# Keys-low product of the second attention's scores over all 128 rows

## The chip, the cores and the metric

The kernel runs on one core of one Trainium2 chip. The metric is the device time of one execution in microseconds (us), the median over the runs shown. TensorE (PE) does the matrix products, VectorE (DVE), ScalarE (ACT) and GpSimd (POOL) the elementwise work, and SyncE (SP) issues the transfers. All matrices are in SBUF, and TensorE writes to the eight banks of PSUM, 512 float32 columns each.

## The reference

The reference is a decoder trunk with two layers on a sequence of 512 tokens, with 1024 channels. Layer one is a causal attention with forget gates, then a squared-ReLU MLP. Layer two is a sliding-window attention that reads one shared set of keys and values, then another such MLP. The change is in layer two's attention. Cut to what matters:

```
q = rmsnorm((h @ w_q).reshape(512, 16 heads, 64), g_q)
k, v = shared keys and values: 2 heads of 64, each read by 8 query heads
s = q . k / sqrt(64) + bias(distance)          # previous block of 128 and the own one
s = -inf outside the window of 128
p = softmax([s, sink])                          # the sink logit is dropped afterwards
o = (p @ v) @ w_out
```

## The kernel before

Nearly all products are made in a rounded float32 format that TensorE takes at full rate. To keep float32 precision, a matrix is held as two parts: *hi* is the rounded value, *lo* the rounded rest. A large product is three of them (function `three`, lines 1210 to 1212): hi by hi, hi by lo, lo by hi. The weight projections and the MLPs are made so, with 512 moving columns each.

**Second attention.** The 16 query heads are done as 8 pairs j = 0 to 7, and a head of a pair is e = 0 or 1. A head has 64 channels, and SBUF has 128 partitions, so the two parts of one head share a tile. `q_hl[:, e, :]` holds the hi part of head e's queries on the 64 rows `own`, which are rows 0 to 63 for e = 0 and 64 to 127 for e = 1, and the lo part on the 64 others. `kd_hi[:, g, :]` holds the hi part of key head g twice, on both halves of the rows, and `kd_lo[:, g, :]` the lo part twice, likewise.

**Scores** (`swa_scores`). For head e there are four key blocks kb of 128 keys. Each has 256 queries, and the last has 128. The scores of a key block are the sum of five products in PSUM: keys hi by queries hi and lo at once over 128 rows (line 1554), keys lo by queries hi over 64 rows (line 1555), minus the row maximum through a diagonal matrix (line 1556), and the bias in two parts (lines 1557, 1558). After the four blocks, one product of 512 columns (line 1561) puts the maximum into bank 6 + e and signals `swa_scores_done`. It may write this bank only after the output of the previous pair's head has been taken from it (`swa_out_stored`, set by DVE on line 1173).

**Order on PE.** The order is written out by hand. For each pair j it is: `swa_max_scores(j)` (rough scores over 64 rows, lines 1532 to 1539, for the row maximum), the projection of pair j+2 (`swa_proj`, 24 products of 512 columns and 2 of `swa_sum`), `swa_scores(j)`, `swa_pv(j)` (probabilities by values, line 1570, 7 products of 128 columns for each head; the trace merges the 14 products of a pair and their 14 weight loads into one row of x28). In pairs 6 and 7 there is no projection left, and a piece of 12 products of the output projection (`out_piece`) stands in its place. In pair 0 half of a projection stands there.

**Other engines.** DVE does for pair j: the row maxima (`swa_max`, lines 1147 to 1153), the diagonal matrix of each head (line 1157, `swa_diag_ready`), the end of the previous pair's reciprocal (lines 990, 993), the previous pair's output (line 1173, one instruction for each head), the norm of a later pair's queries (lines 830, 833, 1106), then the lo part of the next queries (line 1114) and the denominators (line 1166). ACT does the exponentials of head 0 and head 1 after each `swa_scores_done` (lines 738, 739, 741), and with the last of them lets `swa_pv` begin. Then it makes the hi part of the next queries (line 731), the start of the reciprocal (lines 596, 598) and, after pairs 1, 3 and 5, the hi part of a weight unit (line 469), whose lo part POOL makes (line 410).

Weights come in units of 1 MB through two slots. Each transfer, hi part and lo part waits for the use of a unit before it.

Of the kernel before, what the change touches and what calls it, by code (L numbers as in the profile page):

```python
# [90 lines left out]
def build(nc, x, g_attn, g_mlp, w_in_a, b_f, gq_a, gk_a, w_out_a, g_kv, w_kv, gk_b,  # L91
          w_q_b, gq_b, sinks, rel_bias, w_out_b, w_up, w_down, consts, out):
    with ExitStack() as ctx:
# [6 lines left out]
        def at(name, shape, dt, offset):  # L100
            assert offset + 4 * int(np.prod(shape[1:])) <= limit, (name, offset, limit)
            return nc.alloc_sbuf_tensor_at(name, shape, dt, offset=offset)
# [83 lines left out]
        q_hl = at("q_hl", [P, 2, T], F32R, area + 61 * KB)  # L186
        kd_hi = at("kd_hi", [P, 2, T], F32R, area + 65 * KB)
        kd_lo = at("kd_lo", [P, 2, T], F32R, area + 69 * KB)
# [111 lines left out]
        def after(eng, s, count):  # L300

            if not (isinstance(count, int) and count <= 0):
                eng.wait_ge(s, count)
# [901 lines left out]
        def _(pe):  # L1205
            mm = nc.tensor.matmul
# [27 lines left out]
            for v in range(4):  # L1234
# [7 lines left out]
                for k in range(KC):  # L1242
# [19 lines left out]
                    for b in range(TB):  # L1262
                        o = ps[:, V_BANKS[v] + b // 2, 256 * (b % 2):256 * (b % 2) + 256]
# [278 lines left out]
            def swa_scores(j):  # L1542
                g = j // (PAIRS // 2)
                pe.wait_ge(swa_lo_ready, j + 2)
                for e in range(2):
                    pe.wait_ge(swa_diag_ready, 2 * j + e + 1)
                    b = 2 + 2 * e
                    h = slice(64 * e, 64 * e + 64)
                    for kb, bank, c0 in ((0, b, 0), (1, b, 256), (2, b + 1, 0), (3, b + 1, 256)):
                        n = 2 * P if kb < TB - 1 else P  # L1550
                        o = ps[:, bank, c0:c0 + n]
                        ks, qs = slice(kb * P, (kb + 1) * P), slice(kb * P, kb * P + n)

                        mm(o, kd_hi[:, g, ks], q_hl[:, e, qs], start=True, stop=False)
                        mm(o, kd_lo[h, g, ks], q_hl[h, e, qs], start=False, stop=False)  # L1555
                        mm(o, ones_r[:], swa_diag[:, e, qs], start=False, stop=False)  # L1556
                        mm(o, anti_r[:], hk_lo[:, 2 * j + e, 0:n], start=False, stop=False)  # L1557
                        mm(o, anti_r[:], hk_hi[:, 2 * j + e, 0:n], start=False, stop=True)

                    after(pe, swa_out_stored, 2 * j - 1 + e)  # L1560
                    mm(ps[:, 6 + e, :], ones_r[:], swa_diag[:, e, :], start=True, stop=True).then_inc(swa_scores_done, 1)
# [21 lines left out]
            for j in range(PAIRS - 1):  # L1583
                swa_max_scores(j)
                if j == 0:
                    swa_proj(2, False, (2, 6), range(4, KC))
                elif j + 2 < PAIRS:
                    swa_proj(j + 2, False, (j + 2, 2))
                if j == 6:
                    pe.wait_ge(swa_raw_ready, PAIRS + 1)  # L1590
                    out_piece(1, 0, range(1), range(0, 4))
                    swa_sum(PAIRS)
                if j == 0:
                    pe.wait_ge(swa_v_ready, 1)
                    pe.wait_ge(hankel_lo_ready, 1)
                if j == PAIRS // 2:
                    pe.wait_ge(hankel_lo_ready, 2)
                swa_scores(j)
                swa_pv(j)
            swa_max_scores(PAIRS - 1)  # L1600
            pe.wait_ge(swa_rstd_refined, 2 * PAIRS + 1)
            out_piece(1, 0, range(1, 2), range(0, 4))
            swa_scores(PAIRS - 1)
            swa_pv(PAIRS - 1)
            out_piece(1, 0, both, range(4, 7))
# [44 lines left out]
```

## Time and profile before

| | |
|---|---|
| device time, median of 3 runs | 1274.31 us (1271.7 to 1276.66) |
| span of the profiled execution | 1267.8 us |
| PE busy | 1226.4 us, 97% of the span |
| DVE, ACT, POOL busy | 576.1, 478.2, 558.5 us |
| mean granted TensorE clock over the span | 0.984 of full |

The span runs from the first to the last instruction of the profiled execution. The profile gives no device time of that execution; what lies around the span is taken as 1274.31 - 1267.8 = 6.5 us. The granted clock is a share of 2.4 GHz, so 1.00 is 2.4 GHz and 0.50 is 1.2 GHz. The ends of matmuls are modelled, and consecutive ones overlap in the trace, so the pace of TensorE is read from one start to the next, not from durations.

### The profile page before, as it was taken

What the parts mean: (1) busy time and instruction counts of PE and PEld (TensorE: products, weight loads), DVE (VectorE), ACT (ScalarE), POOL (GpSimd) and SP (SyncE); (2) the same over time, 40 slices, a digit from 0 to 9 for tenths busy, and PEclk for the clock granted to TensorE, in tenths of its full rate; (3) what the DMA queues carried; (4) which work ended last, traced back from release to release, by engine and by line L of the source; (5) the groups of instructions that cost most, each with busy time, mean ns of one, the idle gap of its engine ahead of it and who ended that gap; (6) DMA issues with size and microseconds to landing.
All of it is one profiled execution on the core that took longest, in us unless ns stands there. A gap on an engine that the chain in (4) does not pass through costs nothing.

```text
span 1267.8 us, 15311 instructions
## 1 busy us (share of the span) xinstructions
PE 1226.4 (97%) x5794; PEld 1010.5 (80%) x5794; DVE 576.1 (45%) x717; ACT 478.2 (38%) x594; POOL 558.5 (44%) x383
## 2 busy tenths in 40 slices
PE   6999999999999999999999799999999999999998
PEld 6877877777888888888887678777788888888887
DVE  5857778867533001333116676866743200133100
ACT  4248778753322112222227244443332211222221
POOL 4513423415655444565445320221655544566532
PEclk9999999999999999999999699989999999999999
DMA  6221211112333353333333101110333333323341
GB/s 219 80 66 34 55 45 33 59 41 69 99 99 99 100 166 99 94 92 83 97 99 100 34 1 33 34 34 1 100 100 99 100 100 99 91 89 92 103 116 42
DMA packets 142238, 101.24 MB, mean 80 GB/s; under 512 B 3128, under 2 KB 141552, under 8 KB 142192
## 3 DMA queue, kind: packets, MB, share of 16 engines
q1 hardware_dynamic: 142128, 100.56, 26.8%
q8 instruction: 32, 0.52, 0.2%
q14 instruction: 14, 0.11, 0.0%
q10 hardware_dynamic: 64, 0.03, 0.0%
HBM read 98.47 MB, written 2.12 MB: 79 GB/s over the span
## 4 chain that ended last, share of the span: by engine, by line
PE 68%; issue 15%; DVE 7%; POOL 6%; ACT 3%; DMA 0%; SPq 0%; POOLq 0%; ACTq 0%; DVEq 0%
PE ps L1210 21%; PE ps L1212 21%; PE ps L1211 21%; POOL w_lo L410 5%; POOL fox_sq_lo L417 1%; PE ps L1556 1%; PE ps L1555 1%; DVE xn_lo L854 1%; DVE rst L826 1%; DVE x_hat L847 1%; DVE swa_diag L1157 1%; PE ps L1570 1%; ACT w_hi L469 1%; DMA x_in<-in_x 0%; PE ps L1557 0%
## 5 line engine op out<-in xcount | busy, mean ns | idle before, releaser
L410 POOL TENSOR_TENSOR w_lo<-stage,w_hi 128x512 fp32r<-128x512 f32 x356 | 519.9, 1490 | 487.8 <-ACT w_hi L469 480.2
L469 ACT ACTIVATE w_hi<-stage 128x2048 fp32r<-128x2048 f32 x88 | 168.4, 1914 | 475.2 <-PE ps L1212 470.4
L1210 PE MATMUL ps<-xn_hi,w_hi 128*128 128x512 f32 x720 | 285.3, 396 | 0.3 <-issue 0.3
L1212 PE MATMUL ps<-xn_hi,w_lo 128*128 128x512 f32 x720 | 281.0, 390 | 0.0
L1211 PE MATMUL ps<-xn_lo,w_hi 128*128 128x512 f32 x720 | 280.9, 390 | 0.0
L1210 PE MATMUL ps<-r_hi,w_hi 128*128 128x512 f32 x512 | 199.8, 390 | 0.0
L1212 PE MATMUL ps<-r_hi,w_lo 128*128 128x512 f32 x512 | 199.3, 389 | 0.0
L1211 PE MATMUL ps<-r_lo,w_hi 128*128 128x512 f32 x512 | 199.2, 389 | 0.0
L1210 PEld LDWEIGHTS ps<-xn_hi,w_hi 128*128 128x128 f32 x720 | 135.5, 188 | 30.6 <-issue 2.7
L1211 PEld LDWEIGHTS ps<-xn_lo,w_hi 128*128 128x128 f32 x720 | 135.5, 188 | 29.2 <-issue 1.9
L1212 PEld LDWEIGHTS ps<-xn_hi,w_lo 128*128 128x128 f32 x720 | 135.4, 188 | 28.6
L1035 DVE TENSOR_TENSOR hT<-hT,ps 128x512 f32 x40 | 26.8, 685 | 231.5 <-PE ps L1212 231.5
L1057 DVE SCALAR_TENSOR_TENSOR qkn<-ps,rst 128x1024 f32<-128x1024 f32 x32 | 39.2, 1225 | 186.3 <-PE ps L1212 185.8
L1212 PEld LDWEIGHTS ps<-r_hi,w_lo 128*128 128x128 f32 x512 | 96.1, 188 | 20.2
L1211 PEld LDWEIGHTS ps<-r_lo,w_hi 128*128 128x128 f32 x512 | 96.1, 188 | 19.8
L1210 PEld LDWEIGHTS ps<-r_hi,w_hi 128*128 128x128 f32 x512 | 96.1, 188 | 19.7
L417 POOL TENSOR_TENSOR fox_sq_lo<-sqt,fox_sq_hi 128x512 fp32r<-128x512 f32 x14 | 20.6, 1474 | 105.7 <-ACT fox_sq_hi L556 105.5
L1064 DVE TENSOR_TENSOR r_lo<-sqt,r_hi 128x1024 f32 x32 | 52.6, 1643 | 19.0 <-ACT r_hi L675 18.7
L417 POOL TENSOR_TENSOR swa_sq_lo<-sqt,swa_sq_hi 128x512 fp32r<-128x512 f32 x6 | 7.9, 1316 | 94.8 <-ACT swa_sq_hi L714 94.8
L826 DVE TENSOR_TENSOR rst<-rst,sqt 128x512 f32<-128x512 f32 x32 | 41.3, 1289 | 17.3 <-ACT sqt L479 16.7
L854 DVE SCALAR_TENSOR_TENSOR xn_lo<-hT,gains,xn_hi (+1 forms) x40 | 47.7, 1204 | 1.8 <-ACT xn_hi L506 1.8
L479 ACT ACTIVATE sqt<-hT 128x512 f32 (+1 forms) x32 | 19.7, 622 | 71.7 <-DVE hT L1035 65.8
(208 smaller groups left out, 1716.9 us busy)
## 6 DMA issues: line engine op xcount, KB each, us to landing
stage<-in_w_up SPq DMA_DIRECT2D x32, 1024.0 KB, 5.5
stage<-in_w_down SPq DMA_DIRECT2D x32, 1024.0 KB, 5.7
stage<-in_w_in_a SPq DMA_DIRECT2D x16, 512.0 KB, 5.0
stage<-in_w_in_a SPq DMA_DIRECT2D x4, 1024.0 KB, 6.2
stage<-in_w_out_a SPq DMA_DIRECT2D x4, 1024.0 KB, 5.2
stage<-in_w_q_b SPq DMA_DIRECT2D x4, 1024.0 KB, 5.1
stage<-in_w_out_b SPq DMA_DIRECT2D x4, 1024.0 KB, 5.2
x_in<-in_x SPq DMA_DIRECT2D x4, 512.0 KB, 7.3
```

The source lines that it names most:

```text
L410: ins = nc.gpsimd.tensor_tensor(w_lo[:, s, c], stage[:, s, c], w_hi[:, s, c].bitcast(F32), ALU.subtract)
L417: nc.gpsimd.tensor_tensor(lo[:], sqt[:, t, :], hi[:].bitcast(F32), ALU.subtract).then_inc(split, 1)
L469: nc.scalar.activation(w_hi[:, s, :], stage[:, s, :], ACT.Copy).then_inc(w_hi_ready, 1)
L479: nc.scalar.activation(sqt[:, slot, :], src, ACT.Square).then_inc(norm_squared, 1)
L826: V.tensor_tensor(acc, acc, sqt[:, slot, :], ALU.add).then_inc(norm_accumulated, 1)
L854: V.scalar_tensor_tensor(out=one[2], in0=one[0], scalar=gains[:, bass.ds(8 * GAIN[fill] + c, 1)], in1=one[1].bitcast(F32), op0=ALU.mult, o ...
L1035: V.tensor_tensor(dst, dst, ps[:, bank, :], ALU.add).then_inc(h_written, 1)
L1057: V.scalar_tensor_tensor(out=qkn[:], in0=ps[:, 2 * j:2 * j + 2, :], scalar=0.0, in1=scale, op0=ALU.max, op1=ALU.mult).then_inc(u_ready, 1)
L1064: V.tensor_tensor(r_lo[:, bass.ds(2 * i, 2), :], sqt[:], r_hi[:, bass.ds(2 * i, 2), :].bitcast(F32), ALU.subtract).then_inc(r_lo_ready, 1)
L1210: mm(out_, st_hi, mv_hi, start=start, stop=False)
L1211: mm(out_, st_hi, mv_lo, start=False, stop=False)
L1212: return mm(out_, st_lo, mv_hi, start=False, stop=stop)
```

## The change

The second of the five products of a key block, keys lo by queries, takes all 128 rows of both tiles instead of the 64 rows of head e's hi queries. Its sum then also has keys lo by queries lo. The number of instructions stays, as do the columns, all tiles, all waits and signals. The slice `h` is no longer needed in this function.

```diff
                 for e in range(2):
                     pe.wait_ge(swa_diag_ready, 2 * j + e + 1)
                     b = 2 + 2 * e
-                    h = slice(64 * e, 64 * e + 64)
                     for kb, bank, c0 in ((0, b, 0), (1, b, 256), (2, b + 1, 0), (3, b + 1, 256)):
                         n = 2 * P if kb < TB - 1 else P
                         o = ps[:, bank, c0:c0 + n]
                         ks, qs = slice(kb * P, (kb + 1) * P), slice(kb * P, kb * P + n)
 
                         mm(o, kd_hi[:, g, ks], q_hl[:, e, qs], start=True, stop=False)
-                        mm(o, kd_lo[h, g, ks], q_hl[h, e, qs], start=False, stop=False)
+                        mm(o, kd_lo[:, g, ks], q_hl[:, e, qs], start=False, stop=False)
                         mm(o, ones_r[:], swa_diag[:, e, qs], start=False, stop=False)
                         mm(o, anti_r[:], hk_lo[:, 2 * j + e, 0:n], start=False, stop=False)
                         mm(o, anti_r[:], hk_hi[:, 2 * j + e, 0:n], start=False, stop=True)
```

## Rows read from the trace of the kernel before

**Rows 1.** The page: busy time by engine, and the chain that ended last by engine.
```profile
PE 1226.4 (97%) x5794; PEld 1010.5 (80%) x5794; DVE 576.1 (45%) x717; ACT 478.2 (38%) x594; POOL 558.5 (44%) x383
...
PE 68%; issue 15%; DVE 7%; POOL 6%; ACT 3%; DMA 0%; SPq 0%; POOLq 0%; ACTq 0%; DVEq 0%
```
**Rows 2.** Line 1555's instructions: ns min/median/max, starts, forms.
```profile
L1555 PE MATMUL ps<-q_hl,kd_lo x64: 322/381/580, 710.6 to 866.0; 64*128 64x256 f32 x48, 64*128 64x128 f32 x16
```
**Rows 3.** Timeline of PE, pair 1 head 0: start us, us, instruction.
```profile
736.46 0.28 PE L1554 MATMUL ps<-q_hl,kd_hi 128*128 128x256 f32 x1
736.66 0.38 PE L1555 MATMUL ps<-q_hl,kd_lo 64*128 64x256 f32 x1
736.97 0.38 PE L1556 MATMUL ps<-swa_diag,ones_r 128*128 128x256 f32 x1
737.19 0.28 PE L1557 MATMUL ps<-hk_lo,anti_r 128*128 128x256 f32 x1
737.31 0.28 PE L1558 MATMUL ps<-hk_hi,anti_r 128*128 128x256 f32 x1
737.43 0.28 PE L1554 MATMUL ps<-q_hl,kd_hi 128*128 128x256 f32 x1
...
740.19 0.44 PE L1561 MATMUL ps<-swa_diag,ones_r 128*128 128x512 f32 x1
740.47 0.28 PE L1554 MATMUL ps<-q_hl,kd_hi 128*128 128x256 f32 x1
...
744.49 3.63 PE L1570 MATMUL ps<-swa_p,swa_vx 128*128 128x128 f32 x28
```
**Rows 4.** Timeline of PE, scores of the first attention, all 128 rows.
```profile
272.01 0.28 PE L1340 MATMUL ps<-qk_hi 128*128 128x256 f32 x1
272.13 0.28 PE L1341 MATMUL ps<-qk_x 128*128 128x256 f32 x1
```
**Rows 5.** Timeline of PE, pair 0: first product, then `swa_pv`; brackets give idle time before.
```profile
710.14 0.55 PE L1554 MATMUL ps<-q_hl,kd_hi 128*128 128x256 f32 x1 [6.79 <-DVE swa_diag L1157]
...
723.98 4.18 PE L1570 MATMUL ps<-swa_p,swa_vx 128*128 128x128 f32 x28
```
**Rows 6.** Stretches at the low clock: us, busy us (instructions) of PE, clock, DMA.
```profile
57.04:60.10 3.06, 3.06 (x14) 0.50 0.02 5
268.66:271.50 2.84, 2.84 (x9) 0.50 0.00 0
710.14:723.98 13.84, 13.84 (x42) 0.50 0.00 0
```
**Rows 7.** Timeline of DVE: diagonals and outputs in pairs 1, 2 and 7.
```profile
735.50 1.41 DVE L1173 TENSOR_TENSOR o_t<-ps,q_rec 64x512 f32<-64x512 f32 x2
...
754.80 1.74 DVE L1157 TENSOR_TENSOR swa_diag<-kept,nm 128x512 fp32r<-128x512 f32 x1
...
759.96 1.41 DVE L1173 TENSOR_TENSOR o_t<-ps,q_rec 64x512 f32<-64x512 f32 x2
...
860.76 1.41 DVE L1173 TENSOR_TENSOR o_t<-ps,q_rec 64x512 f32<-64x512 f32 x2
```
**Rows 8.** Timeline of PE: line 1561 of head 0 in pairs 2, 6, 7, and pair 6's `swa_pv`.
```profile
760.70 0.50 PE L1561 MATMUL ps<-swa_diag,ones_r 128*128 128x512 f32 x1 [0.40 <-DVE o_t L1173]
...
841.66 0.61 PE L1561 MATMUL ps<-swa_diag,ones_r 128*128 128x512 f32 x1 [3.08 <-DVE o_t L1173]
...
848.93 4.83 PE L1570 MATMUL ps<-swa_p,swa_vx 128*128 128x128 f32 x28
...
862.61 0.44 PE L1561 MATMUL ps<-swa_diag,ones_r 128*128 128x512 f32 x1
```
**Rows 9.** Timeline of ACT, pair 1 head 0: the last exponential.
```profile
741.53 0.69 ACT L741 ACTIVATE psink<-ps,sinkb 128x512 f32<-128x512 f32 x1
```
**Rows 10.** Timeline of PE: idle before a product at 1.2 GHz, and before one at 2.4 GHz.
```profile
57.04 0.55 PE L1210 MATMUL ps<-w_hi,xn_hi 128*128 128x256 f32 x1 [2.25 <-DVE v_all L908]
...
888.65 0.47 PE L1210 MATMUL ps<-ob_hi,w_hi 128*128 128x512 f32 x1 [1.75 <-POOL w_lo L410]
```

## The prediction

> **What bounds the kernel now.** I read the page first. TensorE is busy for 97% of the span, the others for less than half, and the chain that ended last lies 68% on TensorE, with another 15% as its issue [rows 1]. So time taken off TensorE counts, if the stage around it has no other limit. Busy time hides how it is spent: matmuls overlap in the trace. Next I took the instructions of the changed line, to count them: 64, of which 48 have 256 columns and 16 have 128 [rows 2]. Then I read the timeline of TensorE through a pair of heads, from start to start, and saw the point of the whole case. Two products over 128 rows that follow each other start 0.12 us apart (line 1557 to 1558, and 1558 to the next block's 1554). Around the 64-row product the distances are 0.20 (1554 to 1555), 0.31 (1555 to 1556) and 0.22 us (1556 to 1557) [rows 3]. One block of five products takes 0.97 us, where five times 0.12 would be 0.60. Last I read who waits within this stage, on DVE and ACT, and the granted clock.
>
> **The change on TensorE at the full clock.** Nothing is added or removed, and no transfer, wait or signal moves. One product in five changes its form. The new form isn't in this place of the trace, but its twin is: in the first attention's scores a product over all 128 rows with 256 columns (line 1341) follows another one 0.12 us later [rows 4]. Bounds for a block of 256: if all three long distances go, it takes 0.60 us and saves 0.37. If 1554 to 1555 stays at 0.20 for another reason, it saves 0.29. If nothing goes, it saves nothing. I take 0.37, by the twin and because the distance that is longest stands behind the 64-row product, not at the columns. I give 128-column blocks 0.12 for each product too, 0.60 in all.
>
> A head now takes 740.47 - 736.46 = 4.01 us, with line 1561's own 0.28 (740.47 - 740.19) [rows 3]. After the change it is 4 x 0.60 + 0.28 = 2.68. So a head saves 1.33 us and a pair 2.66.
>
> A rule against this change is in the Trainium skill, TensorE: Matmul & The Clock Gate, Part 3 (The mechanism): a weight load overlaps matmuls in flight only where it goes to other rows of the array. By it a 64-row load could have overlapped a product on the other rows, and a full one never could. The trace doesn't agree: full products with loads of their own start 0.12 us apart [rows 4]. By the rule the sum would be about 5 us smaller; the rival that has this mechanism is priced from rows below.
>
> **What of it reaches the end, pair by pair.** In `swa_scores` of pair j, line 1561 waits for the output of pair j-1 (DVE, line 1173). This is the wait that could grow.
>
> Pairs 1, 3, 5. Head 0's output is stored at about 736.2 (half of the 1.41 us from 735.50) [rows 7]. Line 1561 started at 740.19 [rows 3] and would come 1.33 earlier, at 738.9. That is 2.7 us of room. The full 2.66 us count in each: 8.0 us.
>
> Pairs 2 and 4. Here POOL splits a weight unit meanwhile, and DVE is slower: the second diagonal took 1.74 us, and the output came at 759.96 [rows 7]. Line 1561 already waited 0.40 us [rows 8]. What head 0 saves goes into that wait, which becomes 0.40 + 1.33 = 1.73 us. DVE's chain hangs on TensorE's pace before the projection, which doesn't change relative to it. The second diagonal is ready at 754.80 + 1.74 = 756.5, before head 1 starts. Head 1 alone counts: 1.33 us in each, 2.7 us in all.
>
> Pair 0. It starts after 6.79 us of idle time at 1.2 GHz, and the 13.84 us from 710.14 to 723.98 all run so [rows 5, 6]. In two other stretches, with products over 128 rows only, TensorE was back at 2.4 GHz 3.06 and 2.84 us after such a start [rows 6]. I expect this of the new scores too. Both heads are 5.36 us of work at full clock. With 3 us at half pace, 1.5 us are lost: 6.9 us instead of 13.84, a gain of 6.9. Then `swa_pv` takes 3.63 as in pair 1, not 4.18 [rows 3, 5]: 0.55. Sum 7.5 us. If the clock stays low as now, a product takes 3.06 / 14 = 0.22 us [rows 6]. Both heads are then near 40 x 0.22 + 2 x 0.5 = 9.8 us, and the gain is 4.0.
>
> Pair 6. Its shorter filling leaves a wait of 3.08 us at line 1561 [rows 8], and head 0's gain goes into it as in pair 2. After the wait, 848.93 + 4.83 - 841.66 = 12.10 us are spent on line 1561, head 1 and `swa_pv` [rows 8], mostly at the low clock. After the change: 0.28 + 2.68 + 3.63 + 1.5 lost to the clock = 8.1. Gain 4.0 us.
>
> Pair 7. Head 0's output was stored at 860.76 + 0.7 = 861.45, and line 1561 started at 862.61 [rows 7, 8]: 1.16 us of room for 1.33 of advance, so 0.17 waits. Pair 6's `swa_pv` also becomes 1.2 us shorter, while DVE behind the exponentials doesn't. I charge 0.4 for that: 2.66 - 0.6 = 2.1 us.
>
> **What could be late next.** The exponentials of head 0 end at 742.22 [rows 9], and `swa_pv` begins at 744.49 [rows 3]. It will begin 1.33 earlier, at 743.2, so 0.9 us remain. Head 1's exponentials are timed by `swa_scores_done`, as is what follows them. Everything after the stage, the transfers too, waits for uses on TensorE and shifts with it.
>
> **Sum.** 7.5 + 8.0 + 2.7 + 4.0 + 2.1 = 24.3 us. The profiled span of 1267.8 becomes 1243.5. The page has no device time of its own for that execution; the median lies 6.5 us above the span, and I leave that as it is: 1274.31 - 24.3 = 1250.0 us.
>
> **The rivals.**
> - *The new waits of 1.73 us in pairs 2 and 4 drop the clock.* An idle time of 2.25 us had 1.2 GHz behind it, one of 1.75 us had not [rows 10]; these are beside the second. Price 1.5 us each: 1253 us. Chance 0.2, beside the forecast.
> - *The new scores don't bring the clock back.* The mixed ones didn't in 13.84 us [rows 6]. Against it stand the two dense stretches. Pair 0 gains 4.0 instead of 7.5, pair 6 about 2 less: 1256. Chance 0.08.
> - *The full-width load can't run ahead,* so that 1554 to 1555 stays at 0.20: 64 x 0.08 = 5.1 us less, 1255. For it: that distance lies before the 64-row product. Against it: rows 4. Chance 0.07.
> - *Another engine sets the pace of more pairs,* so that head 0's gain goes in all and only half of 8.0 remains, with pair 7 at nothing and half of pair 0: 24.3 - 4 - 2 - 4 = 14, 1260. Against it: the 2.7 us of room in odd pairs. Chance 0.05.
> - *The change doesn't do what it says:* the distances come from the place in PSUM or the shared query tile, not the 64 rows. Against it: 1556 touches neither `q_hl` nor `kd_lo` and is 0.31 behind. 1274. Chance 0.04.
> - *Slower: the low clock after the waits doesn't end.* Its place is pairs 2 to 6, from 760 to 841 us. If the wait in pair 2 dropped it and it stayed, 80 us of work would take 40 more: 1250 + 40 = 1290. It decides from 24.3 / 0.5 = 49 us of low clock on. The longest of [rows 6] is 13.84, with the mixed scores that then are gone. Chance 0.02.
>
> **How the numbers follow.** The forecast case has 0.54 and lies at 1248 to 1252, its terms moving by a microsecond or two. The range should also take in the three rivals at 1253 to 1256, which makes 0.89, and the spread of the median, some 2.5 us to each side in the three runs. On the low side, pairs 2, 4 and 7 might lose less, 2 us. I give 1246 to 1258. Over 0.5% is 6.4 us, about what a measurement of this kernel can tell from no change: all cases but the last two are faster by more. Faster 0.94, same 0.04, slower 0.02.
>
> **What would show it.** Right: lines 1554 to 1558 start 0.12 us apart; a head's scores take 2.7 us; the clock is back by 714 in pair 0; line 1561 waits some 1.7 us in pairs 2 and 4, 4.4 in pair 6, and not in 1, 3, 5. Wrong, if 1555 still starts 0.20 behind 1554, if 1556 is still late with no 64-row product ahead of it, or if a low clock stands in pairs 2 to 5. The clock in pairs 0 and 6 is what I am least sure of: it carries some 6 of the 24 us.

## The result, and the profile after

The changed kernel took 1244.02 us (median of 4 runs, 1242.64 to 1248.39) beside 1275.47 us for the kernel before (4 runs). The ratio is 0.9767, with an interval of [0.9741, 0.9794]: 29.7 us less by the ratio, or 2.3% (31.5 between the medians). The forecast was 1250.0 with a range of 1246 to 1258. The direction and the mechanism were right. The time lies 2 us under the range.

The profiled execution after has a span of 1246.5 us and its own time was 1248.39, so 1.9 us lie around the span, not 6.5. It is the slowest of the four runs. From span to span the change saved 21.3 us, by the ratio 29.7. The experiments had to settle that difference as well.

The page after, as [rows 1]:
```profile
span 1246.5 us, 15311 instructions
...
PE 1198.3 (96%) x5794; PEld 1000.0 (80%) x5794; DVE 575.2 (46%) x717; ACT 478.8 (38%) x594; POOL 560.6 (45%) x383
...
PE 68%; issue 14%; DVE 8%; POOL 6%; ACT 3%; DMA 1%; SPq 0%; POOLq 0%; ACTq 0%; DVEq 0%
```
TensorE lost 28 us of busy time and still bounds the kernel. (A correction to what stands ahead: `swa_pv` has x28 in a row because each of its 14 products in plain float32 has two records, 224 in all, and not because of weight loads.) One line of the source went, so the products of the scores are now on lines 1553 to 1557 and the last one on 1560.

The timeline of TensorE in pair 1, as [rows 3]:
```profile
730.70 0.28 PE L1553 MATMUL ps<-q_hl,kd_hi 128*128 128x256 f32 x1
730.81 0.28 PE L1554 MATMUL ps<-q_hl,kd_lo 128*128 128x256 f32 x1
730.93 0.28 PE L1555 MATMUL ps<-swa_diag,ones_r 128*128 128x256 f32 x1
731.05 0.28 PE L1556 MATMUL ps<-hk_lo,anti_r 128*128 128x256 f32 x1
731.17 0.28 PE L1557 MATMUL ps<-hk_hi,anti_r 128*128 128x256 f32 x1
731.29 0.28 PE L1553 MATMUL ps<-q_hl,kd_hi 128*128 128x256 f32 x1
...
732.49 0.22 PE L1553 MATMUL ps<-q_hl,kd_hi 128*128 128x128 f32 x1
...
733.00 0.45 PE L1560 MATMUL ps<-swa_diag,ones_r 128*128 128x512 f32 x1
...
735.59 0.45 PE L1560 MATMUL ps<-swa_diag,ones_r 128*128 128x512 f32 x1
```
All three long distances are gone: 0.11 or 0.12 us from start to start. A block of 256 queries takes 0.59 us, for 0.97 before. The block of 128 takes 0.51 (732.49 to 733.00), where I had allowed 0.60, and a head takes 2.59 (733.00 to 735.59), not 2.68. So a head saves 1.42 us, not 1.33.

The waits of the last scores product for DVE's output, as [rows 8]. These are head 0 of pairs 2, 4, 6 and 7:
```profile
752.09 0.50 PE L1560 MATMUL ps<-swa_diag,ones_r 128*128 128x512 f32 x1 [1.84 <-DVE o_t L1173]
...
788.34 0.71 PE L1560 MATMUL ps<-swa_diag,ones_r 128*128 128x512 f32 x1 [1.84 <-DVE o_t L1173]
...
826.04 0.79 PE L1560 MATMUL ps<-swa_diag,ones_r 128*128 128x512 f32 x1 [4.51 <-DVE o_t L1173]
...
842.67 0.50 PE L1560 MATMUL ps<-swa_diag,ones_r 128*128 128x512 f32 x1 [1.01 <-DVE o_t L1173]
```
What head 0 saved stands there as waiting: 0.40 became 1.84 in pair 2, 3.08 became 4.51 in pair 6, 1.4 more in each. Pair 7 had none and has 1.01. Pair 4, which had 0.37, has the same 1.84 as pair 2.

The low clock after, as [rows 6], in custom stretches (us, busy and count for PE, PEld, DVE, ACT, POOL, then the clock):
```profile
706.50:716.60 10.10, 5.71 (x26) 5.65 (x27) 8.94 (x10) 0.64 (x2) 3.69 (x1) 0.50 0.30 104
788.80:792.00 3.20, 3.20 (x17) 3.15 (x16) 2.95 (x5) 1.56 (x3) 0.00 (x0) 0.52 0.89 305
826.00:829.70 3.70, 3.66 (x17) 3.57 (x18) 2.83 (x4) 1.56 (x3) 0.00 (x0) 0.54 0.86 286
```
In pair 0 the scores began at 710.89 at 1.2 GHz, and the clock was back at 716.6, after 5.7 us. Before, it had stayed low for all 13.84 us of the scores [rows 5, 6]. In pair 6 it was back 3.7 us after the wait. Pair 4 is new: after the wait of 1.84 us the clock fell, while after the same wait in pair 2 it did not.

### The profile page after: what moved, and what is told of

It reads as the page before. It is cut to its first block, busy times and chain, and to the rows that moved or that the text cites. A ratio compares the mean times of both kernels' runs of the same rounds, so it can differ in the third digit from the quotient of the medians.

```text
span 1246.5 us, 15311 instructions
## 1 busy us (share of the span) xinstructions
PE 1198.3 (96%) x5794; PEld 1000.0 (80%) x5794; DVE 575.2 (46%) x717; ACT 478.8 (38%) x594; POOL 560.6 (45%) x383
## 4 chain that ended last, share of the span: by engine, by line
PE 68%; issue 14%; DVE 8%; POOL 6%; ACT 3%; DMA 1%; SPq 0%; POOLq 0%; ACTq 0%; DVEq 0%
PE ps L1210 21%; PE ps L1211 21%; PE ps L1212 21%; POOL w_lo L410 5%; POOL fox_sq_lo L417 1%; DVE xn_lo L854 1%; DVE rst L826 1%; DVE x_hat L847 1%; DVE swa_diag L1157 1%; ACT w_hi L469 1%; DMA x_in<-in_x 1%; PE ps L1223 0%; PE ps L1554 0%; PE ps L1556 0%; PE ps L1569 0%
## 5 line engine op out<-in xcount | busy, mean ns | idle before, releaser
L830 DVE SCALAR_TENSOR_TENSOR sqt<-ps,sqt 128x512 f32<-128x512 f32 x29 | 20.0, 688 | 53.8 <-ACT sqt L565 35.1
```

What stands on the lines that cost most here:

```text
L830: V.scalar_tensor_tensor(out=square, in0=mean_square, scalar=EPS, in1=square, op0=ALU.add, op1=ALU.mult).then_inc(refined, 1)
```

## Experiments

All ratios are to runs of the kernel before on the same chip; 1% is 12.7 us. In the edits, the kernel named is the one that is changed.

**1. The kernel before again.** No edit.

> The kernel before, unchanged, to see what its runs spend beyond its profiled execution (span 1267.8 us, clock 0.984). The changed kernel's profiled run took 1.9 us more than its span, so the profiled execution of before took about 1269.7 us, under each of its timed runs (1271.7 to 1276.66). Theory A, the extra time is TensorE at the low clock behind the mixed 64-row and 128-row scores: runs of 1272 to 1277 us, each microsecond over 1269.7 comes with 2 us more of low clock, so the mean clock falls by 0.0008 for each, to about 0.979 at 1276 us. Theory B, it is something else, a transfer or the other engines: the clock stays at 0.984 whatever the time. Theory C: what lies around the span differs by run and is some 6 us here, not 1.9.

Its 12 runs have a median of 1272.56 us (1268.3 to 1276.77), and 17 runs beside it 1272.38. The profile again has a span of 1267.8, a clock of 0.984 and the same low stretches, and this execution took 1269.61 us. So theory C is out: 1.8 us lie around the span. The profiled execution was quick, by some 3 us, but my first median (1275.47 of 4 runs) was as far off the other way.

Between A and B the runs themselves decide, as each has a mean granted clock beside its time. Over the 63 runs of this kernel in these comparisons:

| mean clock | runs | mean time, us |
|---|---|---|
| 0.979 | 5 | 1276.4 |
| 0.981 | 13 | 1274.1 |
| 0.983 | 24 | 1272.3 |
| 0.984 | 10 | 1270.5 |
| 0.985 | 8 | 1270.0 |
| 0.986, 0.987 | 3 | 1268.4 |

The clock falls by some 0.0008 for each microsecond more, which is what theory A said; by theory B it would have stayed at 0.984. So the longer executions are those with more time at the low clock. Where in the kernel they have it isn't shown, as both profiles are of short ones.

**2. The four 64-row products together.** The kernel before, the order changed within a head (the edit is shortened here; all five products of a block are kept):

```diff
-for kb, bank, c0 in blocks:
-    mm(o, kd_hi[:, g, ks], q_hl[:, e, qs], start=True, stop=False)
-    mm(o, kd_lo[h, g, ks], q_hl[h, e, qs], start=False, stop=False)
-    ... three more
+for part in range(3):
+    for kb, bank, c0 in blocks:
+        part 0: mm(o, kd_hi[:, g, ks], q_hl[:, e, qs], start=(c0 == 0), stop=False)
+        part 1: mm(o, kd_lo[h, g, ks], q_hl[h, e, qs], start=False, stop=False)
+        part 2: the three others; the last has stop=(c0 == 256)
```

> The 64-row product is kept, but the four of a head stand together, so TensorE goes from 128 rows to 64 and back once for a head, not four times. Theory 1, each change of the number of rows costs time: three quarters of the distance above 0.12 us goes, a head takes 4.01 - 1.0 = 3.0 us at full clock, and some three quarters of the change's gain is there: 1252 to 1256 us. Theory 2, the 64-row product itself is slow, or its weight load is: nothing gained, 1275 us. Theory 3, only the products in the same block wait for each other's write to the same place in PSUM: also a gain here, but then lines 1554 to 1555 come at 0.12 us each and there is no long distance left at the two places where the rows change.

Ratio 0.983 [0.9807, 0.9854], 1250.41 us: 21.6 us less than before, with the same 64-row products, and 1.6 us under what theory 1 expected. The timeline of TensorE, pair 1 head 0 (x4 are the four products of a head in one row; the starts are what counts):
```profile
728.44 0.58 PE L1555 MATMUL ps<-q_hl,kd_hi 128*128 128x256 f32 x4
728.94 0.68 PE L1557 MATMUL ps<-q_hl,kd_lo 64*128 64x256 f32 x4
729.55 0.39 PE L1559 MATMUL ps<-swa_diag,ones_r 128*128 128x256 f32 x1
729.78 0.28 PE L1560 MATMUL ps<-hk_lo,anti_r 128*128 128x256 f32 x1
729.89 0.28 PE L1561 MATMUL ps<-hk_hi,anti_r 128*128 128x256 f32 x1
...
731.29 0.57 PE L1555 MATMUL ps<-q_hl,kd_hi 128*128 128x256 f32 x4
```
A head takes 2.85 us (728.44 to 731.29), beside 4.01 before and 2.59 after the change. The four 64-row products take 0.61 us in all, the way back to 128 rows included. The cost lies in each going over from 128 rows to 64 and back, some 0.37 us for 256 columns (0.20 + 0.31 + 0.22, where three times 0.12 would do). One of them is left, which costs the head 0.26 us more than none: at 729.55 the next product still comes only 0.23 later. That is theory 1. By theory 2 nothing would have been gained, and by theory 3 no long distance would be left where the rows change. The Trainium skill names a cause: TensorEngine Tiling (Array Packing), Key Properties, says that changing the tiling mode drains the engine, while another tile of the same mode doesn't. The trace agrees in that the cost follows the number of changes; that it is a drain, the distances can't show.

**3. Some pairs alone.** The kernel before, with `r = slice(0, P) if ... else h` for the rows of the product: in pairs 0 and 6, then in all the others.

```diff
-    mm(o, kd_lo[h, g, ks], q_hl[h, e, qs], start=False, stop=False)
+    r = slice(0, P) if j in (0, 6) else h        # the other kernel: j not in (0, 6)
+    mm(o, kd_lo[r, g, ks], q_hl[r, e, qs], start=False, stop=False)
```

> The change in pairs 0 and 6 alone, those that ran at the low clock in the profile of before. By that profile: pair 0 gains 7.5, pair 6 gains 4.0, so 11.5 us less than before on this chip, 1264. If before's runs lose more to the low clock in these pairs than its profile shows: 13 to 18 us less. If the low clock comes back later by itself in the pairs left mixed: under 10 us less.

> The change in pairs 1 to 5 and 7, those that ran at the full clock. By the distances: 2.66 us in each of pairs 1, 3, 5, 1.33 in 2 and 4, 2.1 in 7, so 12.8 us less than before on this chip, 1262.5. If the unexplained 6 us between the medians sit in these pairs (a low clock there in most runs of before, though not in the profiled one): 17 to 20 us less. Both partial gains should add up to the whole one, 30 us, if pairs don't act on each other.

Pairs 0 and 6: ratio 0.989 [0.9867, 0.9913], 14.0 us. The others: 0.9877 [0.9858, 0.9896], 15.6 us. They are 2.5 and 2.8 us above my terms of 11.5 and 12.8. The first term lies inside its interval (11.1 to 16.9 us), the second just below its own (13.2 to 18.1). A new thing is in the profile with only pairs 0 and 6 changed. Pair 4's wait was as short as before, and still the clock went low behind it and stayed so for most of the mixed scores and of `swa_pv`. The wait and the stretch, in two views of that kernel:
```profile
791.55 0.51 PE L1562 MATMUL ps<-swa_diag,ones_r 128*128 128x512 f32 x1 [0.41 <-DVE o_t L1173]
```
```profile
792.00:802.00 10.00, 10.00 (x50) 8.73 (x48) 4.33 (x7) 5.40 (x10) 0.19 (x1) 0.66 0.28 96
```
A mean clock of 0.66 over 10 us is 6.8 us at half pace. The same wait had 0.37 us in the kernel before, and there the clock held. Mixed scores can thus be hit outside pairs 0 and 6, behind a short wait too, which no profile of before showed. Whether this is the surplus of 2.5 us was not shown.

**4. The idle time before pair 0 filled.** Into each kernel, ahead of pair 0's scores; the results aren't used:

```diff
 if j == 0:
+    for _ in range(24):
+        mm(ps[:, 6, :], ones_r[:], xn_hi[:, 0, :], start=True, stop=True)
     pe.wait_ge(swa_v_ready, 1)
```

> The kernel before, with 24 products of 512 columns into an unused bank in the idle 6.8 us ahead of pair 0's scores; their results are not used. They keep TensorE busy at no cost of their own. Theory A, the low clock in pair 0 comes from that idle time and the mixed scores only fail to bring it back: the mixed scores now run at 2.4 GHz throughout, 8.0 us for 13.8 and 3.6 for 4.2 after them, some 6 us less than before. Theory B, the mixed scores bring the clock down by themselves: it falls within pair 0, and 0 to 3 us are gained.

> The same 24 products in the changed kernel, results not used. Pair 0 started at the low clock and had it for 5.9 us in the profile, so 2 to 3 us less than the changed kernel if the clock is kept. Set against before_warm, it gives the change's worth without pair 0's low clock: the distances alone, 2.7 us there; so the change would be worth some 29.7 - 6 + 2.5 = 26 us with the products in both.

The kernel before with the products: ratio 0.9963 [0.9945, 0.9981], 4.7 us less (6.0 from median to median, 1266.15 us beside 1272.14). Pair 0's scores, mixed as ever, ran at the full clock. The first and the last product, then the stretch around them:
```profile
707.68 0.35 PE L1554 MATMUL ps<-q_hl,kd_hi 128*128 128x256 f32 x1 [0.41 <-DVE swa_diag L1157]
...
715.50 0.45 PE L1561 MATMUL ps<-swa_diag,ones_r 128*128 128x512 f32 x1
```
```profile
702.00:726.00 24.00, 23.51 (x129) 18.97 (x128) 17.23 (x26) 8.92 (x16) 6.30 (x3) 1.00 0.14 44
...
832.00:846.00 14.00, 13.09 (x55) 11.00 (x55) 6.24 (x10) 4.24 (x8) 0.00 (x0) 0.57 0.23 76
```
The scores took 8.11 us (707.68 to 715.79, where `swa_pv` began), not 13.84, and the clock is 1.00. So in pair 0 the idle time brought the clock down, and the mixed scores kept it where they began at the full clock. That they can never lose it doesn't follow: in experiment 3 the clock fell in pair 4's mixed scores, 1.7 us behind a wait of 0.41 us. Once it is down, they hold it there: in pair 6 of this execution it was low for most of 14 us. This execution is the quickest of the 12. Three others took 1269.7 to 1273.95 us at mean clocks of 0.985 to 0.983, so it need not stand for all.

The changed kernel with the products: 0.9779 [0.9754, 0.9804] beside 0.9804 [0.9775, 0.9832] without. The clock stayed up in pair 0 there too, and was low for some 3 us in each of pairs 2, 4 and 6. I expected 2 to 3 us; the 3 us between the ratios are inside the intervals. With the products in both kernels the change is worth 21 us between the medians and 23 by the ratios, where I had expected 26.

**5. The changed kernel again, twice.** No edit.

> The changed kernel, unchanged. Two measurements disagree on it: from profile to profile it saved 21.3 us of span (1267.8 to 1246.5), and from median to median 0.0233 of the time, 29.7 us. The two partial changes gave 0.0110 and 0.0123, together 0.0233. Theory A, the profile of before was a quick execution and that of the change a slow one, as the low clock fell: ratio again 0.975 to 0.979, median near 1243, and a second profile under 1246.5 us with less than the 27 us of low clock of the first. Theory B, the first median was the lucky one: ratio 0.981 to 0.984, 1250 us.

> The changed kernel a third time, to settle its size. The first two ratios were 0.9767 and 0.9804, the ten runs have a median of 1245.6 us, and the 50 runs of before so far have 1272.3. Theory A, the truth lies between: ratio 0.977 to 0.981, some 26.5 us. Theory B, one of the two was right: under 0.9765 or over 0.981.

Ratios 0.9804 [0.9775, 0.9832] and 0.981 [0.9788, 0.9832], medians 1246.64 and 1247.96. The three profiles of this one kernel have spans of 1246.5, 1242.8 and 1248.1 us, with mean clocks of 0.990, 0.993 and 0.986. In the second the clock held in pair 4 through a wait of 1.83 us. In the third it fell in pairs 2 and 4. The windows of the second (pair 4, then pair 0's scores), then of the third (pairs 2 and 4):
```profile
785.00:789.00 4.00, 3.38 (x27) 3.29 (x28) 3.87 (x6) 1.82 (x4) 0.00 (x0) 1.00 0.82 260
708.59:716.11 7.52, 7.52 (x43) 7.38 (x44) 4.54 (x9) 1.56 (x3) 0.00 (x0) 0.67 0.00 0
```
```profile
753.00:757.00 4.00, 4.00 (x22) 3.90 (x22) 2.32 (x4) 1.46 (x4) 0.00 (x0) 0.57 0.54 192
790.00:794.00 4.00, 4.00 (x22) 4.00 (x21) 3.02 (x5) 1.56 (x3) 0.00 (x0) 0.57 0.68 236
```
So the same program, with the same 9.2 us of waiting at line 1560, spans 5.3 us of difference, and where the clock falls differs by execution. Over all comparisons, 15 runs of the changed kernel have a median of 1247.4 us (mean 1246.6) and 67 of the kernel before 1272.2 (mean 1272.4). The change is worth 25 to 26 us. The first repetition fell between its two theories: the second profile was quicker, with less low clock, as theory A had it, but the ratio of 0.9804 lies just above A's. The second repetition lies on A's upper border.

**6. One head of each pair.** The edit of experiment 3, with `e == 0` or `e == 1`.

> The change for head 0 of each pair alone. If what head 0 saves goes into the wait at line 1561 in pairs 2, 4, 6 and mostly in 7, only pairs 0, 1, 3, 5 count: 3 times 1.4 us, and 2 to 5 in pair 0, together 7 to 9 us less than before, ratio 0.993 to 0.9945. If the wait hangs on something that comes earlier by itself: all eight heads count, 13 us, ratio under 0.990.

> The change for head 1 of each pair alone. It has no growing wait before it: 7 times 1.4 us, pair 0 and the low clock in pairs 0 and 6 another 4 to 8, together 14 to 18 us less than before, ratio 0.986 to 0.989, and with head 0 alone it should add up to the whole, 26 us. If heads are alike: 13 us each.

Head 0 alone: 0.9953 [0.9934, 0.9972], 6.0 us. Head 1 alone: 0.986 [0.9842, 0.9879], 17.8 us. Together 23.8 us, about the whole. The waits with head 0 alone, then with head 1 alone:
```profile
PE ps L1562 <- DVE o_t L1173: 8.3, 4, 4.5
```
```profile
PE ps L1562 <- DVE o_t L1173: 3.9, 3, 3.1
```
Head 0's work shrank by the same 1.4 us in each pair, but 4.4 us of it turned into waiting (3.9 us before). Head 1's left the waits as they were. Head 0 came out 1 us below the lower end that I had given: its own profile has the low clock in pairs 2, 4 and 6 behind the grown waits, where the mixed scores of head 1 follow. Its windows in pairs 2 and 4:
```profile
754.00:761.00 7.00, 7.00 (x27) 5.97 (x27) 1.98 (x3) 2.52 (x6) 0.00 (x0) 0.51 0.26 92
795.00:806.00 11.00, 11.00 (x46) 9.68 (x46) 4.57 (x7) 5.16 (x10) 0.72 (x1) 0.53 0.22 79
```

**7. POOL's work moved away from DVE's.** The changed kernel, ACT's split of a weight unit moved:

```diff
 swa_rstd(j + 2)
+if j in (2, 4, 6):
+    split_q(2 + j // 2)
 ...
 swa_rec(j)
-if j % 2 == 1:
-    split_q(3 + j // 2)
```

> The changed kernel with ACT's split of a weight unit after pairs 1, 3, 5 moved to just before the next pair's exponentials, some 5 us later; POOL's part moves with it, away from DVE's second diagonal and reciprocal. Theory A, the waits at the last scores product of pairs 2, 4, 6 (1.84, 1.84, 4.51 us) come from DVE's slowed instructions beside POOL: the first two go, the third falls to 1.5 to 2 us, and the clock doesn't fall in pair 4: 6 to 9 us less than the changed kernel, 1235. Theory B, DVE is slow there whatever POOL does, or POOL's later part now delays something else: within 2 us of the changed kernel.

> The changed kernel with both: the 24 products with unused results in the idle time before pair 0, and the later split of weight units. The split alone gave 1234.2 us, the products 1 to 2 us beside the changed kernel. If the two are independent: 1232 to 1233, ratio 0.969. If the low clock before pair 0 only moves to another idle time: 1234 again.

The moved split alone: 1234.22 us, ratio 0.9707 [0.9683, 0.9731], 12 us less than the changed kernel's 1246.64 beside it. Its waits, the stage's only two, are in pairs 6 and 7:
```profile
812.67 0.50 PE L1560 MATMUL ps<-swa_diag,ones_r 128*128 128x512 f32 x1 [0.55 <-DVE o_t L1173]
...
828.69 0.50 PE L1560 MATMUL ps<-swa_diag,ones_r 128*128 128x512 f32 x1 [1.54 <-DVE o_t L1173]
```
DVE's second diagonal and the two steps of the reciprocal beside POOL's subtraction, in pair 2 of the changed kernel and, with the split moved, in pair 2 again:
```profile
744.85 5.92 POOL L410 TENSOR_TENSOR w_lo<-stage,w_hi 128x512 fp32r<-128x512 f32 x4 [3.51 <-ACT w_hi L469]
...
746.21 1.74 DVE L1157 TENSOR_TENSOR swa_diag<-kept,nm 128x512 fp32r<-128x512 f32 x1
747.87 1.77 DVE L990 SCALAR_TENSOR_TENSOR qkn<-qkn,q_rec 128x512 f32<-128x512 f32 x1
749.68 1.64 DVE L993 SCALAR_TENSOR_TENSOR q_rec<-qkn,q_rec 128x512 f32<-128x512 f32 x1
```
```profile
741.51 0.69 DVE L1157 TENSOR_TENSOR swa_diag<-kept,nm 128x512 fp32r<-128x512 f32 x1
742.12 0.69 DVE L990 SCALAR_TENSOR_TENSOR qkn<-qkn,q_rec 128x512 f32<-128x512 f32 x1
742.84 0.69 DVE L993 SCALAR_TENSOR_TENSOR q_rec<-qkn,q_rec 128x512 f32<-128x512 f32 x1
...
743.93 5.91 POOL L410 TENSOR_TENSOR w_lo<-stage,w_hi 128x512 fp32r<-128x512 f32 x4 [6.38 <-ACT w_hi L469]
```
POOL now starts when the reciprocal is done, 3 to 4 us later than it did, counted from the pair's first diagonal (2.9 us in pairs 2 and 4, 4.2 in pair 6). The waits of 1.84 us in pairs 2 and 4 are gone, the one in pair 6 fell from 4.51 to 0.55, more than forecast, and no low clock is left between pairs 1 and 7. Pair 7's wait grew from 1.01 to 1.54. Of the 12 us, 7.1 are waits (9.2 to 2.1 in all). In pair 6 the stretch from line 1560 to `swa_pv`, mostly at the low clock in the changed kernel's profile beside it (0.54), went from 4.9 us (821.80 to 826.70) to 2.9. That makes 9.1 of the 10.3 us between these two spans (1242.8 and 1232.5). The moved split alone beats both kernels.

With the 24 products added: 0.9716 [0.9698, 0.9734], 1233.80 us, no further gain that can be told. Its profile has what the last of the expectations named. Pair 0's scores are at the full clock, and it is low in pair 7 instead, behind the same wait of 1.54 us that left it up without the products:
```profile
826.15 0.50 PE L1560 MATMUL ps<-swa_diag,ones_r 128*128 128x512 f32 x1 [1.54 <-DVE o_t L1173]
```
```profile
826.65:830.32 3.67, 3.67 (x21) 3.67 (x20) 1.47 (x3) 1.56 (x3) 0.00 (x0) 0.54 0.02 4
```
That is one profile of each kernel; whether the products move the low clock in most executions isn't shown.

## Why the prediction was wrong in its number and right in its parts

**The mechanism held.** The long distances went, as the twin in the first attention said. Of the bounds for a block, 0.37 us saved was right (0.97 to 0.59). The Trainium skill, TensorE: Matmul & The Clock Gate, Part 3 (The mechanism), has the rule that a weight load overlaps matmuls in flight only where it goes to other rows. It doesn't hold here: line 1554 with a load of all 128 rows, 0.19 us long, starts 0.11 us behind 1553. The same section of the Trainium skill also has loads that go ahead into a background weight buffer. The prediction's "a full one never could" therefore said more than the section does. No run here shows which way the loads take. The rivals of the unmoved 0.20 us, of no effect, and of a slower kernel are out.

**The split by pairs held.** From the first scores product of pair 0 to pair 7's last one of head 1, 866.63 - 710.14 = 156.5 us before became 845.31 - 710.89 = 134.4 in the changed kernel: 22.1 us. The 0.75 us by which pair 0 began later make it 21.3. My terms against this profile:

| | forecast us | measured us | |
|---|---|---|---|
| pair 0, with `swa_pv` | 7.5 | 6.5 | scores 7.89 us, not 6.9: the clock took 5.7 us to return, not 3 |
| heads that count in full | 1.33 | 1.42 | the 128-query block was costed 0.09 too high |
| wait in pairs 2, 4 | 1.73 | 1.84, 1.84 | the clock fell once, 1.5 us lost in pair 4 |
| pair 6, line 1561 to the end of `swa_pv` | 12.1 to 8.1 | 12.1 to 8.1 | 826.04 to 830.45 + 3.64 |
| wait in pair 7 | 0.6 | 1.01 | 0.17 with pair 6 left as before (experiment 3), the rest by pair 6's shorter scores and `swa_pv` |

The rival of the clock falling in pairs 2 and 4 came true in half of its chances: not at all in the second profile, once in the first, twice in the third. The slower rival didn't come, and its price was too low: 80 us of work at half pace takes 80 us more, not 40, so it stood for 1330 us and not 1290.

**The step that failed** is the last: "the median lies 6.5 us above the span, and I leave that as it is: 1274.31 - 24.3 = 1250.0 us", with "the spread of the median, some 2.5 us to each side". I took the difference between one profiled execution and three runs as a constant around the span. It is 1.8 us; the other 4.7 were a quick execution beside a slow median of three. The spread was counted for one kernel, not for both, and on the low side not at all: 1248, less 2.5 for the median, less 2 for the pairs that might lose less, is 1243.5, where I gave 1246. In the end the 24.3 us of the sum stand beside 25 to 26 from 15 and 67 runs, so the sum was some 1 us small (0.6 by the medians, 1.5 by the means). The block of 128 queries alone explains 0.09 us x 12 heads = 1.1 us. With before at its 1272.2 the forecast would have been 1247.9, and the changed kernel's 15 runs have 1247.4. The first four runs of it at 1244.0 were quick, and the four of before at 1275.5 slow: that was the luck of the draw on both sides. The whole sets give 1247.4 / 1272.2 = 0.9805, where the first comparison had 0.9767.

**Still open.** Where the longer executions of the kernel before have their low clock, and what decides whether it falls. That they have more of it is shown, for both kernels: the changed kernel's runs go from 1241.9 to 1242.7 us at a mean clock of 0.994 (four runs) to 1250.4 to 1251.3 at 0.987 (three). Of the 5.3 us between its quickest and its longest profile, 2.4 lie between the first scores of pair 0 and the last of pair 7, and 3.0 ahead of them. The two profiles of before agree with each other, and no longer execution of it was profiled. The two sets of pairs add up to 29.6 us and the two heads to 23.8, where the whole is 25 to 26: the intervals, 2 to 3 us each, allow both.

## What to carry to other kernels

Read TensorE's pace from start to start. A product over fewer rows between full ones costs more than its columns: here some 0.37 us for going there and back once. Give it all rows if the extra term does no harm, or put such products side by side, which gave most of the gain (21.6 of 25 us). Then look for who takes the gain. Here DVE's output kept head 0's share in three pairs, in which POOL's subtraction slowed it, and most of it in a fourth. Moving POOL's work by 3 to 4 us was worth another 12. Before a forecast in microseconds, ask whether the profiled execution is typical: compare its own time and mean clock with those of the runs, give the spread of both medians to the range, and add every term that you name to both of its ends.

## What the runs showed of the hardware that was not expected

- Products over 64 and 128 rows in turn don't only run slower. Once the clock is at 1.2 GHz, they hold it there: 13.84 us in pair 0 of the kernel before, most of 14 us in pair 6 with the filled idle time. The scores over 128 rows had it back after 3.7 and 5.7 us. Begun at 2.4 GHz, the mixed ones kept it in most pairs (8.1 us in pair 0, filled), but lost it in one, 1.7 us behind a wait of 0.41 us (experiment 3).
- The same wait of 1.83 or 1.84 us dropped the clock in some executions and not in others, and within one execution in pair 4 but not in pair 2. A wait of 1.54 us dropped it in one profile of two.
- The spread between executions of one program goes with the clock: 63 runs of the kernel before, from 1268.1 to 1276.8 us, have a mean clock lower by some 0.0008 for each microsecond more.
- Beside POOL's subtraction into `w_lo`, DVE's diagonal took 1.74 us and the reciprocal's steps 1.77 and 1.64, each 0.69 without it.
